# A chunked linear recurrence: level masks in two buffers, one key product and one addition on GpSimd, VectorE's order changed

## The reference, cut to what matters

```python
def step(S, inp):
    r_t, w_t, kk_t, a_t, k_t, v_t = inp
    sa = jnp.einsum('bhvk,bhk->bhv', S, -kk_t)
    S = S * w_t[:, :, None, :] + sa[..., None] * (kk_t * a_t)[:, :, None, :] + v_t[..., None] * k_t[:, :, None, :]
    return S, jnp.einsum('bhvk,bhk->bhv', S, r_t)
...
o = outs[0] + outs[1]
mu = jnp.mean(o, -1, keepdims=True)
var = jnp.mean(jnp.square(o - mu), -1, keepdims=True)
o = ((o - mu) * lax.rsqrt(var + RWKV_GN_EPS)).reshape(B, T, BRANCH_WIDTH) * p['rwkv_gn_g'] + p['rwkv_gn_b']
bonus = jnp.sum(rh[:, :, None] * k_h * p['rwkv_r_k'], -1, keepdims=True) * vh[:, :, None]
o = o + jnp.sum(bonus, axis=2).reshape(B, T, BRANCH_WIDTH)
return (o * g).astype(cin.dtype), jnp.stack(states, axis=1)
```

## Time and profile before

| | before |
|---|---|
| runs shown, us | 2540.56, 2542.89, 2545.5 (median 2542.89) |
| profiled execution, us | 2548.7 |
| its span, first to last instruction, us | 2545.9 |
| TensorE busy in the span | 2388.8 us, 94% |
| VectorE, ScalarE, GpSimd busy | 1367.8, 1038.2, 332.9 us |
| mean granted TensorE clock | 0.971 of full speed |

### The profile page before, as it was taken

One profiled execution on the slowest core, in us unless ns is written; L12 is line 12 of the kernel. 1 busy time (PEld: TensorE's weight loads), 2 busy tenths in 40 slices (PEclk: granted clock), 3 DMA queues, 4 the chain that ended last, 5 costly groups with the idle time before them and its releaser, 6 DMA issues.

```text
span 2545.9 us, 56113 instructions
## 1 busy us (share of the span) xinstructions
PE 2388.8 (94%) x23644; PEld 2234.5 (88%) x23644; DVE 1367.8 (54%) x2311; ACT 1038.2 (41%) x1686; POOL 332.9 (13%) x326
## 2 busy tenths in 40 slices
PE   6999999999978889999999999999998888899997
PEld 5899989889967779999989899998998777899997
DVE  3434365476478655444443344655766775654444
ACT  3333244355634435333343323434564443353332
POOL 0000032000033304000120002210001341120001
PEclk8999999999999999999999999999999999999998
DMA  8875734233300024563557765333232000334441
GB/s 291 263 221 179 219 93 132 84 94 91 104 7 4 29 62 131 156 188 111 171 184 216 228 192 159 100 108 95 87 87 75 4 4 29 97 106 126 128 131 55
DMA packets 468246, 308.27 MB, mean 121 GB/s; under 512 B 15282, under 2 KB 427420, under 8 KB 467868
## 3 DMA queue, kind: packets, MB, share of 16 engines
q1 hardware_dynamic: 467728, 304.60, 39.9%
q10 hardware_dynamic: 268, 0.09, 0.0%
HBM read 301.25 MB, written 3.41 MB: 120 GB/s over the span
## 4 chain that ended last, share of the span: by engine, by line
PE 85%; DVE 8%; issue 2%; ACT 2%; DMA 1%; POOL 1%; SPq 0%; DVEq 0%; ACTq 0%; POOLq 0%
PE acc L888 22%; PE acc L890 21%; PE acc L889 21%; PE pb L1285 5%; PE acc L1285 2%; PE pb L965 2%; PE pb L973 1%; PE pb L1212 1%; DVE w_lo L2307 1%; PE pb L980 1%; PE pb L888 1%; DMA modx<-in_w_mod 1%; DVE merged L2588 0%; PE pb L1232 0%; DVE gr L2689 0%
## 5 line engine op out<-in xcount | busy, mean ns | idle before, releaser
L888 PE MATMUL acc<-xm_hi,w_hi 128*128 128x384 f32 x2288 | 786.5, 344 | 28.4 <-DVE xm_lo L2317 23.7
L2307 DVE TENSOR_TENSOR w_lo<-raw,w_hi 128x1024 fp32r<-128x1024 f32 (+2 forms) x432 | 531.9, 1231 | 510.6 <-ACT w_hi L1716 502.0
L890 PE MATMUL acc<-xm_hi,w_lo 128*128 128x384 f32 x2288 | 773.4, 338 | 0.0
L889 PE MATMUL acc<-xm_lo,w_hi 128*128 128x384 f32 x2256 | 762.2, 338 | 0.0
L1716 ACT ACTIVATE w_hi<-raw 128x1024 fp32r<-128x1024 f32 (+2 forms) x432 | 446.3, 1033 | 319.6 <-PE acc L890 214.4
L888 PEld LDWEIGHTS acc<-xm_hi,w_hi 128*128 128x128 f32 x2288 | 436.4, 191 | 59.0 <-issue 43.3
L890 PEld LDWEIGHTS acc<-xm_hi,w_lo 128*128 128x128 f32 x2288 | 435.6, 190 | 0.0
L889 PEld LDWEIGHTS acc<-xm_lo,w_hi 128*128 128x128 f32 x2256 | 430.5, 191 | 0.5
L888 PE MATMUL acc<-h_hi,w_hi 128*128 128x384 f32 x704 | 238.8, 339 | 0.0
L890 PE MATMUL acc<-h_hi,w_lo 128*128 128x384 f32 x704 | 237.1, 337 | 0.0
L889 PE MATMUL acc<-h_lo,w_hi 128*128 128x384 f32 x704 | 237.0, 337 | 0.0
(11 more groups left out here) (391 smaller groups left out, 3480.3 us busy)
## 6 DMA issues: line engine op xcount, KB each, us to landing
raw<-in_ffn_w_in SPq DMA_DIRECT2D x176, 512.0 KB, 4.1
modw<-in_w_mod SPq DMA_DIRECT2D x69, 1024.0 KB, 6.7
raw<-in_w_in SPq DMA_DIRECT2D x114, 512.0 KB, 4.1
raw<-in_ffn_w_out SPq DMA_DIRECT2D x64, 512.0 KB, 4.3
raw<-in_w_up SPq DMA_DIRECT2D x24, 512.0 KB, 3.5
raw<-in_ffn_w_out SPq DMA_DIRECT2D x26, 384.0 KB, 3.5
raw<-in_w_out SPq DMA_DIRECT2D x16, 512.0 KB, 4.4
modx<-in_w_mod SPq DMA_DIRECT2D x3, 1024.0 KB, 9.3
```

The lines of the kernel that those rows point to most:

```text
L888: pe.matmul(out, lhs[0], rhs[0], start=first, stop=False)
L889: pe.matmul(out, lhs[0], rhs[1], start=False, stop=False)
L890: return pe.matmul(out, lhs[1], rhs[0], start=False, stop=last)
L2307: done(dve.tensor_tensor(w_lo[:, c % SPL, 0:w], raw[:, c % RAW, 0:w], w_hi[:, c % SPL, 0:w].bitcast(F32), ALU.subtract), lo_done)
```

## The change

- The level masks go to two buffers in turn, `ltm` and `ltm_odd`, so that a mask waits for the multiplication of two levels before, not of the last.
- The product `bt = aa * zi` (one for each tile and direction) goes from VectorE's `prepare_decayed` to the end of GpSimd's `keys`.
- The addition of the bonus to the normalised output goes from VectorE's `tile_out` to GpSimd's `tile_add`, for all tiles but the last. `tile_low` follows the first level's masks of the next turn.
- On VectorE `scan_state(s, 0)` goes ahead of `first_level(j, 0)`, `first_level(j, 1)` ahead of `gram(j, 3)`, `first_level_done(j, 1)` and `scan_state(s, 2)` ahead of `centre_sums(g0)`, `add_ut(j, 5, 1)` and `tile_norm(s)` ahead of `prepare_queries(g1)`.
- `turn_start(j, 1)` writes bank `pb[2]` instead of `pb[1]`, so that it waits for `gram_read` of p = 2, and no longer of p = 3; the first `lx` of the turn has that wait instead. ScalarE's `prepare_decay` loses a wait.

```diff
@@ per_layer
-"gn_taken": 12,
+"gn_taken": 15,
@@ buffers
+        ltm_odd = sb("ltm_odd", [128, 2 * NQ, CH])
-        sb("w_lo_kept2", [128, 2 * 1024 - 2 * TOK])
+        sb("w_lo_kept2", [128, 2 * 1024 - 2 * TOK - 2 * NQ * CH])
+        def masked(j, n):
+            return (ltm, ltm_odd)[(NL * j + n) % 2]
@@ TensorE
 def turn_start(j, d):
-    pe.wait_ge(gram_read, since(l, gram_read, 4 * j + 2 + 2 * d))
+    pe.wait_ge(gram_read, since(l, gram_read, 4 * j + 2 + d))
...
-        mm = quads(pb[d][:, q * CH:(q + 1) * CH], xts[j % 2][:, NQ * d + q, :], id64, True, True)
+        mm = quads(pb[2 * d][:, q * CH:(q + 1) * CH], xts[j % 2][:, NQ * d + q, :], id64, True, True)
@@ TensorE, level_lx0_u1
     if n > 1:
         u_ready(j, n - 1, 1)
+    else:
+        pe.wait_ge(gram_read, since(l, gram_read, 4 * j + 4))
@@ ScalarE, prepare_decay
-    if g >= 2:
-        if j == 1:
-            act.wait_ge(ab_ready, since(l, ab_ready, g - 1))
-        else:
-            act.wait_ge(xt_ready, since(l, xt_ready, 2 * (NL + 1) * (j - 1)))
@@ GpSimd, mask
-    if at >= 2:
-        pool.wait_ge(tl_done, since(l, tl_done, at - 1))
+    if at >= 4:
+        pool.wait_ge(tl_done, since(l, tl_done, at - 3))
...
-    done(pool.tensor_tensor(ltm[:, u, :], lt[:, u, :], over(cst[:, o:o + CH], NQ), ALU.mult), ltm_ready)
+    done(pool.tensor_tensor(masked(j, n)[:, u, :], lt[:, u, :], over(cst[:, o:o + CH], NQ), ALU.mult), ltm_ready)
@@ GpSimd, keys
-    done(pool.tensor_tensor(aa[:, d, :], aa[:, d, :], kk[:, :], ALU.mult), key_ready)
+    link(pool.tensor_tensor(aa[:, d, :], aa[:, d, :], kk[:, :], ALU.mult))
+    pool.wait_ge(exps_done, since(l, exps_done, g + 1))
+    if j >= 1:
+        pool.wait_ge(tok_t, since(l, tok_t, 4 * (j - 1) + 1 + 2 * d))
+    done(pool.tensor_tensor(bt[:, d, :], aa[:, d, :], zi[:, d, :], ALU.mult), key_ready)
+
+def tile_add(j):
+    pool.wait_ge(bonus_read, since(l, bonus_read, j + 1))
+    pool.wait_ge(gn_taken, since(l, gn_taken, 4 * j + 3))
+    pool.tensor_tensor(osum[:, :], osum[:, :], guc[:, 0, :], ALU.add).then_inc(gn_taken, 1)
@@ GpSimd, order
+    if j >= 2:
+        tile_add(j - 2)
     if nxt:
         decay(2 * j + 2)
         decay(2 * j + 3)
     for n in range(1, NL + 1):
         mask(j, n, 0)
         mask(j, n, 1)
+        if n == 1 and j >= 2:
+            tile_low(j - 2)
...
-    if old:
-        tile_low(j - 1)
+tile_add(NB - 2)
+tile_low(NB - 2)
 tile_low(NB - 1)
@@ VectorE
-    link(dve.tensor_tensor(bt[:, d, :], aa[:, d, :], zi[:, d, :], ALU.mult))
     done(dve.tensor_tensor(kt[:, d, :], kt[:, d, :], zi[:, d, :], ALU.mult), ab_ready)
...
-    done(dve.tensor_tensor(xi[:, u, :], pb[d][:, 0:TOK].rearrange("p (q s) -> p q s", q=NQ),
+    done(dve.tensor_tensor(xi[:, u, :], pb[2 * d][:, 0:TOK].rearrange("p (q s) -> p q s", q=NQ),
...
-    dve.wait_ge(gn_taken, since(l, gn_taken, 3 * j + 3))
-    link(dve.tensor_tensor(osum[:, :], osum[:, :], guc[:, 0, :], ALU.add))
+    if j + 1 < NB:
+        dve.wait_ge(gn_taken, since(l, gn_taken, 4 * j + 4))
+    else:
+        dve.wait_ge(gn_taken, since(l, gn_taken, 4 * j + 3))
+        link(dve.tensor_tensor(osum[:, :], osum[:, :], guc[:, 0, :], ALU.add))
@@ VectorE, order
     gram(j, 1)
+    if old:
+        scan_state(s, 0)
     first_level(j, 0)
-    if old:
-        scan_state(s, 0)
     gram(j, 2)
...
+    first_level(j, 1)
     gram(j, 3)
-    first_level(j, 1)
     if old:
         scan_solve(s, 2)
+    first_level_done(j, 1)
+    if old:
+        scan_state(s, 2)
     if nxt:
         centre_sums(g0)
-    first_level_done(j, 1)
-    if old:
-        scan_state(s, 2)
-    if nxt:
         sum_decays(g1)
...
     if old:
         tile_root(s)
+    add_ut(j, 5, 1)
+    if old:
+        tile_norm(s)
     if nxt:
         prepare_queries(g1)
-    add_ut(j, 5, 1)
-    if old:
-        tile_norm(s)
```

More of the change, by code:

```diff
@@ L269, in build @@
         "brc_hi_done": 4, "brc_ready": 4, "cache_in": 64, "chunk_used": NCHUNK, "cmix_ready": 15, "csum_ready": 15,
-        "d_ready": 15, "decay_done": 8, "exp_done": 48, "exps_done": 8, "gn_mean": 4, "gn_moved": 8, "gn_taken": 12,
+        "d_ready": 15, "decay_done": 8, "exp_done": 48, "exps_done": 8, "gn_mean": 4, "gn_moved": 8, "gn_taken": 15,
         "gn_var": 4, "gnr_ready": 4, "gnr_t": 4, "gram_done": 16, "gram_read": 16, "h_ready": 44, "hhi_done": 44,
@@ L1385, in u_ready, with lx_quads @@
                             pe.wait_ge(gram_read, since(l, gram_read, 4 * j + 3))
-                    def lx_quads(n, d, q):
-                        return quads(lx_bank(n, d)[:, q * CH:(q + 1) * CH], ltm[:, NQ * d + q, :], xi[:, NQ * d + q, :],
+                    def lx_quads(j, n, d, q):
+                        return quads(lx_bank(n, d)[:, q * CH:(q + 1) * CH], masked(j, n)[:, NQ * d + q, :], xi[:, NQ * d + q, :],
                                      True, True, d == 1)
@@ L1406, in level_lx0_u1 @@
                             u_ready(j, n - 1, 1)
+                        else:
+                            pe.wait_ge(gram_read, since(l, gram_read, 4 * j + 4))
                         for q in range(NQ):
-                            lx = lx_quads(n, 0, q)
+                            lx = lx_quads(j, n, 0, q)
                             if n > 1:
@@ L1420, in level_u0_lx1 @@
                             uu = u_quads(j, n, 0, q) if n < NL else ut_quads(j, n, 0, q)
-                            lx = lx_quads(n, 1, q)
+                            lx = lx_quads(j, n, 1, q)
                         uu.then_inc(u_done if n < NL else ut_done, 1)
@@ L1539, in tile_var @@
                     def tile_var(j):
-                        pe.wait_ge(gn_taken, since(l, gn_taken, 3 * j + 1))
+                        pe.wait_ge(gn_taken, since(l, gn_taken, 4 * j + 1))
                         for c in range(NCH):
@@ L1994, in tile_square @@
                         act.wait_ge(gn_moved, since(l, gn_moved, 2 * j + 1))
-                        done(act.activation(guc[:, 1, :], osum[:, :], ACT.Square), gn_taken)
+                        act.activation(guc[:, 1, :], osum[:, :], ACT.Square).then_inc(gn_taken, 1)
+                        act.wait_ge(gn_taken, since(l, gn_taken, 4 * j + 1))
                     def tile_std(j):
                         act.wait_ge(gn_var, since(l, gn_var, j + 1))
-                        done(act.activation(gnr[:, :, :].rearrange("p c h -> p (c h)"), acc[2][:, 0:2 * NCH], ACT.Sqrt, scale=1.0 / HD,
-                                            bias=eps[:, 2:3]), gn_taken)
+                        act.activation(gnr[:, :, :].rearrange("p c h -> p (c h)"), acc[2][:, 0:2 * NCH], ACT.Sqrt, scale=1.0 / HD,
+                                       bias=eps[:, 2:3]).then_inc(gn_taken, 1)
+                        act.wait_ge(gn_taken, since(l, gn_taken, 4 * j + 2))
                     def tile_affine(j):
                         act.wait_ge(gn_moved, since(l, gn_moved, 2 * j + 2))
-                        done(act.activation(osum[:, :], osum[:, :], ACT.Identity, scale=par[:, 163 + j:164 + j],
-                                            bias=par[:, 167 + j:168 + j]), gn_taken)
+                        act.activation(osum[:, :], osum[:, :], ACT.Identity, scale=par[:, 163 + j:164 + j],
+                                       bias=par[:, 167 + j:168 + j]).then_inc(gn_taken, 1)
+                        act.wait_ge(gn_taken, since(l, gn_taken, 4 * j + 3))
                     def tile_high(j):
@@ L2768, in tile_root @@
                     def tile_root(j):
-                        dve.wait_ge(gn_taken, since(l, gn_taken, 3 * j + 2))
+                        dve.wait_ge(gn_taken, since(l, gn_taken, 4 * j + 2))
                         done(dve.reciprocal(gnr[:, :, :], gnr[:, :, :]), gnr_ready)
@@ L2819, in _ @@
                         gram(j, 1)
-                        first_level(j, 0)
                         if old:
                             scan_state(s, 0)
+                        first_level(j, 0)
                         gram(j, 2)
@@ L2831, in _ @@
                             sum_decays(g0)
+                        first_level(j, 1)
                         gram(j, 3)
-                        first_level(j, 1)
                         if old:
                             scan_solve(s, 2)
-                        if nxt:
-                            centre_sums(g0)
                         first_level_done(j, 1)
@@ L2841, in _ @@
                         if nxt:
+                            centre_sums(g0)
                             sum_decays(g1)
@@ L2887, in _ @@
                             tile_norm(s)
+                        if nxt:
+                            prepare_queries(g1)
                     ahead(("u", 1, 3))
```

2 lines of the change are left out of this document (removed).

## The result

| kernel | median of the compared runs | ratio to before | 95% interval |
|---|---|---|---|
| before | 2542.51 us (2540.49 to 2546.2, 8 runs) | | |
| changed | 2548.93 us (2544.5 to 2553.93, 8 runs) | 1.0027 | 1.0017 to 1.0036 |

The changed kernel is slower by 0.27%, some 7 us, where I had forecast 2.6 us less. The two together stand near 1.003, about 8 us above before.

What follows compares the result with a forecast made beforehand. The prediction saw TensorE's list as ending the kernel, with each turn a chain around four engines. Per recurrence, +1.8 us at turn 3's start ended at -1.3; -2.6 for both gave 2540.3 us, range 2533 to 2549.5.

Steps and rivals of the forecast that it cites:

- VectorE's order (norm late): First half of turns: scan states and level masks sooner, -0.7 us each in turns 1 and 2; more in turn 3.
- addition on GpSimd, second mask buffer: Bonus addition: VectorE would wait as long as it took itself, 0; mask buffer: TensorE gains nothing directly, 0.
- turn ends: norm ahead, late level 5, less the product: Next turn begins later: +0.6 us after turn 0, +1.3 after turns 1 and 2 each.
- turn 3: product and addition gone: VectorE saves 1.2 us in turn 3, which prepares no next tile; part of that turn's gain.
- Eight products per recurrence leave VectorE: Key products: 0.62 us each off VectorE, about 1.0 us on GpSimd; direction 1's hidden, direction 0's delays level 5.
- Turn 0 has no scan steps: ... I take 0: VectorE's order in turn 0's first half: between -0.3 and +0.75 us, taken as 0.
- the lock: VectorE instructions with two SBUF operands wait out GpSimd's running instruction, costing up to 1.4 us instead of 0.56.
- stands until the spread is done: Turn's end: VectorE reaches the norm 1.3 us sooner and waits for TensorE's spread, with the queries behind it.
- the fast rival: All VectorE is relieved of counts: about 4.5 us per recurrence, 9 for both, 2534 us; chance 0.27.
- VectorE was the bound: In the turns, all relief of VectorE counts: 9 us less for both recurrences, 2534 us; chance 0.27.
- The key step and the lock decide; slower: Level 5 and decay sums: GpSimd filled and forward, VectorE's two-operand instructions come second; +7 us, 2550; chance 0.13.
- Nothing moves: Turn 3's gains and the losses at two turn ends cancel: 2543 us; with the forecast, chance 0.60.

Runs made afterwards that it cites:

- e6: Kernel before with VectorE's new order, norm late, later `tile_low`, `prepare_decay` without its wait; one mask buffer, products and addition on VectorE: 0.9987, 2537.26 us.
- e7: e6 with three of four bonus additions moved to GpSimd: 0.9999.
- e8: e7 with the two level-mask buffers as well: 1.0004.
- e14: e6 with the norm ahead of the queries: 1.0007, 2541.89 us.
- e15: The same text as e6, run again: 0.9993, 2540.38 us.
- e13: Kernel before with the six key products within turns on GpSimd, the two ahead of turn 0 left on VectorE: 0.9998.
- e5: Kernel before with all key products `bt` on GpSimd and nothing else of the change: 1.0002, 2541.41 us.
- e3: Changed kernel with VectorE's last copy and the norm behind the next tile's queries again: 1.0031, 2547.16 us.
- e9: Changed kernel, the same text built and measured a second time: 1.0038, 2550.56 us.
- e4: Changed kernel with direction 0's key product on GpSimd behind level 5's masks instead of ahead: 1.0037, 2549.46 us.
- e12: Changed kernel with the two key products ahead of turn 0 back on VectorE: 1.0012, 2542.47 us.

## Why the prediction was wrong

The steps in order, each from kernel to kernel where two differ by it alone, as differences of ratios times 2541 us:

| part | forecast, both recurrences | measured |
|---|---|---|
| VectorE's order (norm late) | -7 (-0.7, -0.7 and, in turn 3, -1.4 - 0.95 + 0.2; times two) | -3.3, -1.8 |
| addition on GpSimd, second mask buffer | 0 | +2.3 and +1.3, +3.6 together |
| turn ends: norm ahead, late level 5, less the product | +6.4 (0.6 + 1.3 + 1.3, times two) | norm +3.6, +3.0 and 0; six products -1.0, +1.5 and, on the old order, -0.5 |
| turn 3: product and addition gone | -1.8 | in the rows above |
| two products ahead of turn 0 | no term | +3.8, +6.6, +4.3; on the old order +1.0 |

The measured parts add to about +8 us (-2.5 + 3.6 + 2.2 + 0 + 4.9, by their means), which is what the changed kernel shows; each is uncertain by some 3 us, so the agreement is better than it deserves. From the forecast of -2.6 to there it is some 11 us: by these means 4.9 from the start, 4.6 from the order and 3.6 from the addition and the second buffer, less 2.4 by which the rest came out lower than forecast.

**The step that failed: the start.** "Eight products per recurrence leave VectorE" was costed inside the turns only: direction 1's "comes at the end of GpSimd's turn and is needed only in the next: hidden", direction 0's stands "ahead of level 5's masks". Two of the eight are in neither place. They are ahead of turn 0, where VectorE has to wait for GpSimd and TensorE for VectorE. Turn 0 got "Turn 0 has no scan steps: ... I take 0", and the start got no term. The rows were there: 1.0 us on GpSimd for 0.62 on VectorE, no cover, twice. It measured 1.36 us for each start directly, at VectorE's gram and at TensorE alike, and 4 to 7 us in all.

**A term that was too large: the order.** -7 us were forecast and 2.5 measured. Turn 1 gained more than the -0.7: it takes 43.7 us in the first recurrence of e6, e7, e8, e14 and e15, against 45.33 in before and 45.39 in e13. Turn 3 gained less than it seems: 43.47 and 44.20 us in e6 and e15 look like -4 us beside before's 47.75, but before's turn 3 is the one with the fall of the clock. Beside e13's 44.38 they are -0.9 and -0.2. And turn 0, taken as 0, is 0.2 to 0.9 us longer than in e13 in the first recurrence and 0.7 to 0.9 in the second. A part of this goes with the lock. VectorE's 18 instructions that centre and sum the decays take 13.5 to 13.6 us for a recurrence in before, e5 and e13, and 15.2 to 16.0 in all kernels with the new order: some 3.7 us more work over both recurrences that the order has to earn back.

**A term put at nothing: the addition and the second buffer**, 0 forecast and +3.6 us together, with the second buffer's part seen in the decays and the addition's not located.

**The turn ends were right in kind and not too small.** The prediction saw that VectorE "stands until the spread is done", and it does, 0.84 us. With the norm ahead this wait goes from 1.5 to 2.4 us in the first recurrence (e15 to e14). TensorE's wait for the norm was to give back 0.93 us at each of two turn ends and gave 0.25. The other wait at the turn's end, 1.60 us for ScalarE's root, doesn't come from the norm. The same view of waits in e14, norm ahead and products on VectorE, and in e3, norm late and products on GpSimd:

```profile
DVE gnr L2780 <- ACT gnr L2001: 3.1, 2, 1.7
DVE gnr L2786 <- ACT gnr L2001: 5.1, 4, 1.7
```

It is 3.1 us in two waits in every kernel whose direction-0 product within the turns stays on VectorE, before included, and 3.3 to 5.4 us in three or four where GpSimd makes it. So it belongs to the product and the late level 5, whose cost the runs put near nothing.

**Slips in the working.** The two reorderings of 0.6 and 0.97 us make 1.6, not 1.7, and the fast rival's half of all relief is 5 us, not 4.5. Neither moves the forecast by as much as its uncertainty.

**Right.** Level 5 waits for a mask 2.17 us ("1.7 us or more"). The masks of levels run together, and the lock is paid: `sg` and `cs` take 1.24 and 1.63 us. In before's turn 0 they take 0.56 and 1.11 us, and the scan 0.96 where it ran alone. The Trainium skill (SBUF — State Buffer, Who interferes with whom) has it that a VectorE instruction with two SBUF inputs contends with a GpSimd instruction that reads SBUF, and that their shared ports are an exclusive lock; the trace agrees, with 1.63 us for 0.96. Turns 1 and 2 at "45 to 46 us" are 45.4 to 47.2. Turn 3 was to be "some 3 us shorter": without a fall of the clock it takes 41.71 us in e9 and 43.94 in e4, against 44.38 and 44.67 in e13 and e5, so 0.4 to 3 us.

**Rivals.** *VectorE was the bound* fell: it was relieved of 1.6 and 3.2 us in the windows of turns 1 and 2 and of 11.0 us over the span, and the kernel isn't faster. *The key step and the lock decide; slower* gave the number that came near (2550), for another reason. Its test was that VectorE's busy time wouldn't fall, and it fell; and e4, which takes the product out from ahead of level 5, gains nothing in the runs. That its number is close is luck. *Nothing moves* is excluded by the interval of two builds.

**What stays open.** Why the kernels with the new order and the first products on GpSimd have a mean clock 0.002 lower, and e5 hasn't; whether that is the cause of what the direct 2.7 us leave unexplained or goes along with it. Why e4's shorter turns of the first recurrence are hardly there in the second and don't show in its runs. How the 3.6 us of the addition and the second buffer divide. What the norm ahead costs, between nothing and 3.5 us. What of the 2.5 us gained is the order's, and what `tile_low`'s and ScalarE's.

## What to carry to other kernels

When an operation leaves a full engine for a slower one, count each of its places by itself, and first those ahead of the loop: an engine that works its list in order hides a wait only with work that stands ahead of it, and here VectorE's nine other instructions stood behind. Judge a change of a few tenths of a per cent by many runs of the kernel and of its parts, and use a trace for the waits and the lengths of single stretches, each with its granted clock beside it: 3.4 us at the lower level made before's turn 3 look 3 us longer than that of nearly the same list in e13. Two profiled spans can have the wrong sign, here 3.1 us faster for a kernel that is 7 us slower. Taking a part out of the changed kernel and putting it alone into the old one can differ (the first products: 4 to 7 us on the new order, 1 us on the old, with some 3 us of uncertainty), so do both.

## What the hardware showed unexpectedly

The time of this kernel goes with the granted clock even where the list of instructions is nearly the same. The stretch at 1.2 GHz at the start of a recurrence has one of two lengths, 6.8 or 10.2 us; with 1.4 us more of waiting it was the longer one in all 14 starts, and without it, in 12 of 22 on the new order and in all 4 on the old. Over the runs of a kernel the time moves by about 1.3 us for each 0.001 of mean clock. The changed kernel (e9, 0.9720) and e12 (0.9738) differ by four products' engine, and by 7 us, where those four explain 2.7 directly.
